# Expert stage: VectorE copies a result bank behind the first activation half of the next chunk, and ScalarE stores it behind that half's sigmoid

## What is computed

```python
def expert_block(args):
    rows, e = args
    gu = x[rows] @ wgu[e] + bgu[e]
    gt, up = jnp.split(gu, 2, axis=-1)
    gt = jnp.minimum(gt, SWIGLU_LIMIT)
    up = jnp.clip(up, -SWIGLU_LIMIT, SWIGLU_LIMIT)
    return ((up + 1.0) * gt * jax.nn.sigmoid(SWIGLU_ALPHA * gt)) @ wd[e] + bd[e]
```

## Time and profile before

| | |
|---|---|
| time, median of 3 runs | 2740.69 us (2737.85 to 2742.93) |
| the profiled execution's own time | 2746.34 us |
| its span | 2744.6 us |
| TensorE busy with matmuls | 2113.4 us (77%) |
| VectorE busy | 994.5 us (36%) |
| ScalarE busy | 315.8 us (12%) |
| mean granted TensorE clock | 0.783 |
| HBM read and written | 510.14 MB and 25.16 MB |

### The profile page before, as it was taken

How to read it: one execution, slowest core, us unless ns; L and a number is a source line. 1 busy time by engine, 2 the same in 40 slices (tenths; PEclk the granted TensorE clock), 3 DMA queues, 4 the chain that set the end, 5 groups by cost and what they waited for, 6 DMA issues and landing times. The chain is left out here.

```text
span 2744.6 us, 51803 instructions
## 1 busy us (share of the span) xinstructions
PE 2113.4 (77%) x20894; PEld 1326.6 (48%) x20895; DVE 994.5 (36%) x2133; ACT 315.8 (12%) x754; POOL 196.4 (7%) x362
## 2 busy tenths in 40 slices
PE   6799628545888788996955888688888899889661
PEld 1287528443444555665333455355455555555330
DVE  2200375512666383752452222122222222222118
ACT  0000101003222100010000111011111111111000
POOL 0000100003000400000000000000000000000020
PEclk9899769758555555555966999899899999999775
DMA  8521000051000300200407999988998747995973
GB/s 279 197 70 49 11 8 1 2 205 62 1 0 1 153 33 1 123 3 20 151 31 296 416 386 417 408 338 349 417 373 359 279 162 307 417 390 229 417 305 122
DMA packets 130057, 534.12 MB, mean 195 GB/s; under 512 B 11710, under 2 KB 36403, under 8 KB 95301
## 3 DMA queue, kind: packets, MB, share of 16 engines
q1 hardware_dynamic: 110970, 476.37, 43.8%
q0 software_dynamic: 8576, 46.28, 4.3%
q10 hardware_dynamic: 10446, 10.58, 1.2%
HBM read 510.14 MB, written 25.16 MB: 195 GB/s over the span
## 5 line engine op out<-in xcount | busy, mean ns | idle before, releaser
L2352 PE MATMUL ps<-wgu,xTm 128*32 128x256 f32 x10112 | 616.9, 396 | 78.6 <-DMA wgu<-in_moe_wgu 77.3
L2352 PEld LDWEIGHTS ps<-wgu,xTm 128*32 128x32 f32 x10112 | 373.2, 114 | 283.8 <-issue 139.4
L2374 PE MATMUL ps<-wd,aT 128*32 128x256 f32 x5056 | 321.9, 399 | 25.7 <-DMA wd<-in_moe_wd 23.1
L2374 PEld LDWEIGHTS ps<-wd,aT 128*32 128x32 f32 x5056 | 173.6, 114 | 150.1 <-issue 87.5
L2485 DVE COPY orow<-ps 128x256 f32<-128x256 f32 x79 | 33.5, 424 | 539.9 <-DMA outbuf<-orow 483.6
L2465 DVE TENSOR_TENSOR hx<-ps,biasT 128x256 f32<-128x256 f32 x158 | 67.1, 424 | 356.5 <-PE ps L2365 328.7
L348 PE MATMUL ps<-hT,w_ring 128*128 128x260 f32 (+2 forms) x768 | 170.9, 386 | 1.1 <-ACT hT L313 1.1
L348 PEld LDWEIGHTS ps<-hT,w_ring 128*128 128x128 f32 (+2 forms) x768 | 141.1, 184 | 30.7 <-issue 1.5
L2420 ACT ACTIVATE gs<-ps 128x256 f32<-128x256 f32 x158 | 60.1, 380 | 660.1 <-PE ps L2352 660.1
L2365 PE MATMUL ps<-ident,gs 128*128 128x128 f32 x316 | 69.1, 302 | 50.3 <-ACT gs L2420 48.4
L209 PE MATMUL ps<-ada_ring,cT 128*9 128x512 f32 x192 | 87.6, 620 | 13.4 <-DVE mod L231 10.2
(11 more groups left out here) (544 smaller groups left out, 2290.6 us busy)
## 6 DMA issues: line engine op xcount, KB each, us to landing
wgu<-in_moe_wgu SPq DMA_DIRECT2D x128, 2048.0 KB, 24.9
wd<-in_moe_wd SPq DMA_DIRECT2D x64, 2048.0 KB
ada_ring<-in_w_ada SPq DMA_DIRECT2D x12, 2048.0 KB, 8.7
w_ring<-in_w_in SPq DMA_DIRECT2D x10, 1024.0 KB, 5.2
outbuf<-orow ACTq DMA_DIRECT2D x79, 128.0 KB
outbuf<-zero SPq DMA_DIRECT2D x8, 512.0 KB
w_out_s<-in_w_out SPq DMA_DIRECT2D x2, 2048.0 KB, 10.8
xh<-in_x_prompt SPq DMA_DIRECT2D x1, 2048.0 KB
```

Of the source, the lines that this page charges most:

```text
L2352: m = pe.matmul(ps[32 * c:32 * c + 32, p, 0:256].rearrange("r (s n) -> r s n", s=2), xT[:, t, 32 * q:32 * q + 32], wgu[b][:, 2 * q + t, :, ...
L2374: m = pe.matmul(ps[32 * c:32 * c + 32, 6, 0:256], aT[:, k, :], wd[b][:, k, 256 * c:256 * c + 256], start=(k == 0), stop=(k == KD - 1))
```

## The change

VectorE's copy of the result is put into a function `result(g)`, which copies the bank of chunk g - 1. It is called between `activate(0, g)` and `activate(1, g)`, and once more after the loops for the last chunk. The first call, for g = 0, copies what the bank happens to hold, and that copy isn't stored; it takes the place of the initial increment of `r_ev`. ScalarE's `store(g - 1)` moves from before `sigmoid(0, g)` to behind it, still ahead of `evacuate(1, g)`. The copy of chunk g - 1 waits for the landing of the store of chunk g - 2, as before; since there is one copy more, `r_st` starts at 32.

```diff
-            act.sem_inc(r_st, 16)
+            act.sem_inc(r_st, 32)
...
             with act.Fori(1, total) as g:
                 evacuate(0, g)
+                sigmoid(0, g)
                 store(g - 1)
-                sigmoid(0, g)
                 evacuate(1, g)
                 act.wait_ge(x_t, g + 2)
                 turned()
                 sigmoid(1, g)
             store(total - 1)
-            act.wait_ge(r_st, 16 * total + 16)
+            act.wait_ge(r_st, 16 * total + 32)
...
             v.sem_inc(t_rd, 2)
-            v.sem_inc(r_ev, 1)
...
+            def result(g):
+                v.wait_ge(d_mm, 2 * g + 1)
+                v.wait_ge(r_st, 16 * g + 16)
+                v.tensor_copy(orow[:], ps[:, 6, 0:256]).then_inc(r_ev, 1)
+
...
                 with v.Fori(0, N) as j:
                     g = F0 + j
                     activate(0, e, g)
+                    result(g)
                     activate(1, e, g)
-                    v.wait_ge(d_mm, 2 * g + 3)
-                    v.wait_ge(r_st, 16 * g + 16)
-                    v.tensor_copy(orow[:], ps[:, 6, 0:256]).then_inc(r_ev, 1)
+            result(v.value_load(tab[0:1, 0, E:E + 1], min_val=E, max_val=MAX_CH))
```

## The result

The changed kernel takes 2792.04 us (median of 4 runs, 2789.13 to 2792.22) against 2741.43 us: ratio 1.0184, 95% interval 1.0166 to 1.0202. It is slower by 50.6 us, where 52 was forecast. The profiled execution took 2789.13 us, its span is 2787.3 us. The two profiled spans differ by 42.7 us: before the first gate-and-up copy, in stages that the change doesn't touch, the changed kernel is 5.3 us ahead (1480.79 against 1486.11 us), and from that copy to the one of the last chunk the stage grows by 48.5 us.

A forecast was written before the change was run, and what follows sets the result against it. The weight stream and TensorE's own order were taken to bound the expert stage by turns. Issue 44.9, landings 35.1, old waits -31.5, clock 6.4, less 3 coming back, gave +52 us: 2793 us on the median, 2798 profiled, range 2766 to 2824.

The forecast's parts named there:

- The order: In an undisturbed chunk, the store's issue on ScalarE ahead of `evacuate(1)` makes it 1.15 us late: 13.42 us instead of 12.27.
- The open bound: How long a DMA issue holds ScalarE's next instruction: `evacuate(1)` 0.6 us late from below, 1.75 from above, 1.15 taken.
- Rival 1: The store's issue doesn't hold ScalarE up: 23.4 us in place of 44.9, +31 us, 2772 us; chance 0.14.
- The ring: Copy into `orow`, store and landing with one buffer: landings over 12.8 us felt in full, 13 long ones, 35.1 us.
- the five stretches: Parts of the expert stage where TensorE waits for no weights and DMA engines have idle time; 39 chunks, the ones counted.
- Rival 4: Every waiting landing comes out long and TensorE's clock falls each time: +125 us, about 2865 us; chance 0.12.
- rival 3: Faster: late landings no longer meet the activation, landings stay under 12.8 us: -14 us, 2727 us; chance 0.05.
- The clock: TensorE's granted clock falls after long gaps, +1.43 us on the down matmuls; half of nine added gaps, 6.4 us.
- The sum: Over 39 chunks: issue 44.9, long landings 35.1, old waits -31.5, clock 6.4; +54.9 us, less 3, leaves +52 us.
- The cover: The 40 chunks beside TensorE's waits for weights count at nothing, since those 95.5 us of waits cover them.
- Rival 2: The weight stream covers the added time, 91 us fitting into 95.5 us of waits: stays at 2741 us; chance 0.04.
- the larger of: A chunk takes the larger of 13.42 us and the cycle of landing, copy and store, 12.4 or 16.0 us.

## Why the prediction was right

**The order.** Forecast 1.15 us for each undisturbed chunk, measured 13.46 - 12.27 = 1.19. The open bound, whether the issue holds ScalarE, is closed at its middle value: 0.56 us of issue and 0.12 us behind it. The match is a little closer than the reasoning: `evacuate(1)` is 1.08 us late, not 1.15, and 0.11 us is the gap between the down halves, which the sum didn't have. Of the 1.08 us, 0.68 is the issue; the other 0.4 is the wait for the copy ahead of it. The runs show it from three sides: the move behind `evacuate(1)` takes all but 0.12 us away, a second issue adds 0.7 us, and an issue that ends before bank 1 is ready costs nothing. Rival 1 is out. Of the two places in the Trainium skill, "Perfetto Trace Analysis", section "DMA Instruction — HWDGE (DVE, Sync)", agrees with the trace: the next instruction starts 0.12 us behind the shown end. The other page's remark that the issue is small is true of the 0.56 us and no guide to its price. With two buffers the store's place ahead of `evacuate(1)` costs 2758.59 - 2709.57 = 49 us (46 against each one's own kernel before); that includes the wait for the copy and the branch, which stand there with it.

**The ring.** No slack was forecast past 12.8 us of landing, and each late landing is felt in full (2.62 us in the timeline above). In the five stretches 12 copies of the changed kernel wait for a landing, 28.9 us in all (2, 3, 2, 1 and 4 copies; 4.9, 5.8, 5.1, 2.5 and 10.6 us in the waits of VectorE in these windows). Eleven of the 12 wait 2.4 to 3.0 us and one 0.4. I had 12 or 13 at 2.7 us, 32 us. The size follows from the ring; the number was a guess, somewhat under half of 29, and that it came true is luck. One reading was too simple: from two rows I took landings of two kinds, 11.8 and 15.4 us. In the kernel before, the 60 waiting copies start 9.9 to 16.0 us after the issue, with all values between; in the changed kernel 26 of the 30 start 15.4 to 16.0 us after it, since a landing under 12.8 us no longer meets a waiting copy. Rival 4, that most landings would come out long, didn't happen, and rival 3 neither: the landings didn't shorten.

**The clock.** Here the term was undersized. I let half of the nine added long gaps cost a slow spell; all 12 chunks with a late landing have one, the one with a gap of only 1.47 us too, each about 1.3 us (a long chunk takes 17.39 us, which is 13.46 + 2.62 + 1.31; 0.73 granted in the 6 us behind the gap):

```profile
2184.00:2190.00 6.00, 6.00 (x78) 3.05 (x82) 1.53 (x5) 0.40 (x2) 0.00 (x0) 0.73 1.01 408
```

**The sum.** At 12.27 us each, the 41 chunks of the five stretches would take 503.1 us. Before they lost 45.6 us on that, after 96.3. After: 41 x 1.19 = 48.8 for the issue, 28.9 for landings, 12 x 1.3 = 15.6 for the clock, 3 us left over. Before: 31.5 us of waits for `gs`, 5 slow spells at about 1.4, and some 7 us left over, of which the largest part, 2.2 us, is the first chunk of the second stretch, where the granted clock is still 0.68 over 6 us behind a wait for weights. So the issue came out 4 higher than forecast (two chunks more by these edges), the landings 3 lower, the clock 9 instead of 6. The old losses that the change removes were 7 us larger than the 31.5 I took. These partly cancel, and the closeness of 52 to 50.6 owes something to that. It owes something to the executions too: what the traces show is +50.7 in the five stretches and +42.7 between the two profiled spans, while the medians differ by 50.6.

**The cover.** That only the stretches without waits for weights count was right: +50.7 in the five, -2.1 in the rest of the stage. Rival 2, that the stream would hide it, holds for the first stretch (15.2 us in, 15.1 back) and for no other. The waits for weights fell by 67.7 us, further than the 35 I named, and still the time rose; where the loads wait for a buffer that TensorE frees late, a wait for weights is shorter only because TensorE gets there later.

**The two costs are not additive.** On the changed kernel, the issue's removal alone brings 23 us, the ring's alone 33, both 82. A chunk takes the larger of its own order and the ring: taking one away leaves the other. Of the 26 us by which both together bring more than the sum of the two, up to 16 can be the branches: they cost 0.4 us in each of the 41 chunks where two buffers go with the store ahead of `evacuate(1)`, and nothing where the store stands behind `turned`. I had this in the prediction as "the larger of", and yet added the two rows of savings when I forecast the store behind `turned`, at 2752 instead of 2769.

What stays open is why landings are long and short by turns, and what decides between a gap of 1.4 us with and without a slow spell. Neither was tried.

## What to carry to other kernels

Before a DMA issue is moved on a compute engine's queue, look at what stands behind it there: half a microsecond of issue behind a wait for another engine is charged to every instruction after it, and if one of them feeds the busiest engine it is paid in each turn of the loop. With one buffer between a copy and its store, count the ring (landing, copy, issue) against the period and ask how much slack the places in the loop leave; moving the wait later gains nothing if the issue moves later by the same. Where the ring is near the period, try a second buffer: here it beat every order with one buffer, 1% faster than the kernel before, provided that the issue stood where its engine waits anyway. With the issue ahead of `evacuate(1)` it was still 0.6% slower.

## What the runs showed of the hardware

With idle gaps of 1.4 to 1.5 us in every chunk, TensorE's granted clock fell behind 6 of 41 of them, to 0.70 over the next 5.7 us, and stayed at 1.00 behind the others. With gaps of 2.1 to 2.3 us in nearly every chunk it fell behind 20 of 41. Each spell costs 1.3 to 1.4 us.

A DMA issued from ScalarE holds the next activation for 0.68 us from its start, and two in a row for 1.55 us (2205.39 to 2206.94), with 0.16 us between them.
